# The first group's tokens gathered by halves, and eight instead of six step places in a layer's first expert pair

## What is computed

```
aff  = sigmoid(x @ router_w)                    # 16 experts in 4 groups of 4
g    = argmax of the groups' sum of their two best (aff + bias)
e    = the two best experts within group g; gate = aff[e] / sum(aff[e])
h    = silu(x @ w_gate[e]) * (x @ w_up[e]) * gate      # w_gate, w_up: 2048 x 512
out  = sum over the two experts of h @ w_down[e]       # w_down: 512 x 2048
x    = layer_norm(alpha * x + out)
```

## Time and profile before

| what | value |
|---|---|
| median of 3 runs | 1759.06 us (1756.92 to 1761.03) |
| the profiled execution | 1759.79 us, its span 1757.9 us |
| TensorE matmul busy | 1596.2 us, 91% |
| weight loads of TensorE | 948.4 us, 54% |
| VectorE, ScalarE, GpSimd busy | 720.8, 467.4, 16.8 us |
| moved by DMA | 538.12 MB, mean 306 GB/s |
| TensorE's mean granted clock | 0.977 of full |

### The profile page before, as it was taken

The page is one execution under the profiler, slowest core; times in us unless marked ns, Lnnn a source line. Parts: engine busy times, 40 slices in busy tenths (PEclk is TensorE's granted clock), DMA queues, the critical chain, the costliest instruction groups (busy, mean ns, idle before and its releaser), DMA issues.

```text
span 1757.9 us, 18363 instructions
## 1 busy us (share of the span) xinstructions
PE 1596.2 (91%) x7223; PEld 948.4 (54%) x7223; DVE 720.8 (41%) x1220; ACT 467.4 (27%) x693; POOL 16.8 (1%) x36
## 2 busy tenths in 40 slices
PE   8999999998999879898879999999799988989985
PEld 6888887876533224333237888878543323533321
DVE  6675555656211112111157797656521112111116
ACT  4565545432110001000024335553220000100000
POOL 1000000000000000000000000000000000000000
PEclk9999999998999999999999999999899999999998
DMA  8666554784899999999994555538489999999995
GB/s 267 174 180 182 166 158 141 262 310 157 319 416 421 421 416 422 419 422 421 421 361 120 168 167 162 162 121 347 175 354 421 421 421 416 421 415 422 421 419 234
DMA packets 133270, 538.12 MB, mean 306 GB/s; under 512 B 19377, under 2 KB 19505, under 8 KB 86849
## 3 DMA queue, kind: packets, MB, share of 16 engines
q1 hardware_dynamic: 132608, 532.75, 80.0%
q0 software_dynamic: 576, 4.19, 0.6%
HBM read 534.82 MB, written 2.10 MB: 305 GB/s over the span
## 4 chain that ended last, share of the span: by engine, by line
PE 56%; issue 29%; DMA 10%; DVE 3%; ACT 1%; SPq 1%; POOL 0%; POOLq 0%; DVEq 0%; ACTq 0%
PE ps L750 12%; PE ps L752 11%; PE ps L751 11%; PE ps L1035 8%; DMA ring<-in_moe_w_down 5%; PE ps L1097 4%; DMA ring<-in_moe_w_up 4%; PE ps L731 2%; PE ps L1015 1%; PE ps L1016 1%; PE ps L1024 1%; PE ps L1208 1%; PE ps L1222 1%; DMA arena<-in_x 0%; SPq L597 0%
## 5 line engine op out<-in xcount | busy, mean ns | idle before, releaser
L750 PE MATMUL ps<-w_lo,x_hi 128*128 128x512 f32 x880 | 350.7, 399 | 7.5 <-DVE x_lo L2312 2.5
L751 PE MATMUL ps<-w_hi,x_hi 128*128 128x512 f32 x880 | 344.7, 392 | 0.0
L1768 DVE TENSOR_TENSOR w_lo<-ring,w_hi 128x1024 fp32r<-128x1024 f32 x224 | 270.2, 1223 | 181.2 <-ACT w_hi L1315 179.6
L1315 ACT ACTIVATE w_hi<-ring 128x1024 fp32r<-128x1024 f32 x224 | 235.5, 1059 | 311.5 <-PE ps L752 306.8
L2210 DVE TENSOR_TENSOR arena<-ps,arena 128x512 f32<-128x512 f32 x128 | 82.9, 687 | 418.7 <-PE ps L1025 418.7
L750 PEld LDWEIGHTS ps<-w_lo,x_hi 128*128 128x128 f32 x880 | 166.5, 189 | 46.3 <-issue 7.2
L1035 PE MATMUL ps<-arena,hT 128*64 128x512 f32 x768 | 177.1, 616 | 9.6 <-DVE hT L2200 4.3
L751 PEld LDWEIGHTS ps<-w_hi,x_hi 128*128 128x128 f32 x880 | 166.5, 189 | 34.7 <-issue 0.5
L1097 PE MATMUL ps<-ring,arena 128*64 128x512 f32 x768 | 170.5, 594 | 6.4 <-DMA ring<-in_moe_w_down 6.4
L1524 ACT ACTIVATE y_hi<-ps 128x512 fp32r<-128x512 f32 x64 | 36.1, 596 | 459.9 <-PE ps L1097 239.7
L752 PE MATMUL ps<-w_hi,h_lo 128*128 128x512 f32 x384 | 150.2, 391 | 0.0
(11 more groups left out here) (333 smaller groups left out, 1530.8 us busy)
## 6 DMA issues: line engine op xcount, KB each, us to landing
arena<-in_moe_w_gate SPq DMA_DIRECT2D x48, 2048.0 KB, 18.3
ring<-in_moe_w_down SPq DMA_DIRECT2D x96, 1024.0 KB, 18.2
arena<-in_moe_w_up SPq DMA_DIRECT2D x32, 2048.0 KB, 20.4
ring<-in_moe_w_up SPq DMA_DIRECT2D x32, 2048.0 KB, 20.7
ring<-in_ab_w_in SPq DMA_DIRECT2D x96, 512.0 KB, 3.7
ring<-in_moe_w_gate SPq DMA_DIRECT2D x16, 2048.0 KB, 19.9
arena<-in_moe_w_down SPq DMA_DIRECT2D x32, 1024.0 KB, 17.1
ring<-in_c_w_in SPq DMA_DIRECT2D x64, 512.0 KB, 3.7
```

What stands on the lines that cost most here:

```text
L750: nc.tensor.matmul(t, x_h, w_l[:, k, :], start=(opens and k == 0), stop=False)
L751: nc.tensor.matmul(t, x_h, w_h[:, k, :], start=False, stop=False)
L1315: act.activation(high_unit(n), raw_unit(n)[0], ACT.Copy).then_inc(w_hi_ready, 1)
L1768: v.tensor_tensor(lo, raw, high_unit(n).bitcast(FP32), ALU.subtract).then_inc(w_lo_ready, 1)
```

## The change

Four edits, made together.

1. **Two more step places in a layer's first pair.** Steps 6 and 7 get places of their own in `arena` (words 0 to 4095 and 4096 to 8191); the steps after them go to place `(st - 2) % 6`. Steps 0, 7, 1 and 2 are loaded between the out projection's units, step 3 (layer 1: 4) after unit -5, and 4 (layer 1: 3), 5 and 6 after the last. Steps 0 and 1 of the second pair wait for steps 4 and 5 of the first instead of 6 and 7.
2. **The first group is gathered by halves.** 16 tiles with 256 columns for the first four experts go into `first_pairs` (all of `hT`); 16 tiles for the other four (`gather_rest`) go into `other_pairs` (words 0 to 4095 of `arena`, step 6's place): eight after the first pair's projections, and two before each two projections of the second pair.
3. **Picks by halves.** VectorE makes the picks of the first four experts first (`pick_first`), the others after `low(1, .)`; the first pair's picks are turned behind the second gather tile instead of before the first. A tile waits for its own token half of `h_lo`.
4. **Other homes.** The LayerNorm is done in place in `h`; the two vectors of the LN lie where `h_hi` will be; `acc` is formed later by VectorE as `h_hi + h_lo` (`acc_joined`) and scaled then by ScalarE. `mix_lo`, `attn_lo`, `rawT` and `rparts` move, and layer 1's units begin four slots later in `ring`, so that units 0 to 3 of layer 1 wait for step 6 of the last pair and units 4 to 7 for its step 11.

```diff
+        def opening(x):
+            return isinstance(x, int) and x == 0
+        def slot_of(x, st):
+            return st if opening(x) and st < 6 else (st - 2) % 6
...
-                if not (isinstance(x, int) and x == 0 and st < 6):
-                    sp.wait_ge(M[lay]["step_used"], STEPS * x + st - 5)
+                if not opening(x):
+                    sp.wait_ge(M[lay]["step_used"], STEPS * x + st - (7 if isinstance(x, int) and x == 1 and st < 2 else 5))
+                elif st >= 8:
+                    sp.wait_ge(M[lay]["step_used"], st - 7)
...
-                    if n in (UNITS[lay] - 12, UNITS[lay] - 8, UNITS[lay] - 4):
-                        sp.wait_ge(mix_ready if lay == 0 else mixer1_done, 1)
-                        load_step(lay, 0, 0, (n - UNITS[lay] + 12) // 4)
+                    if n in (UNITS[lay] - 12, UNITS[lay] - 9, UNITS[lay] - 6, UNITS[lay] - 3):
+                        load_step(lay, 0, 0, (0, 7, 1, 2)[(n - UNITS[lay] + 12) // 3])
+                early, late = (3, 4) if lay == 0 else (4, 3)
                 wait_unit_used(sp, lay, UNITS[lay] - RAW + 3)
-                load_step(lay, 0, 0, 3)
+                load_step(lay, 0, 0, early)
                 wait_unit_used(sp, lay, UNITS[lay] - 1)
-                for st in range(4, STEPS):
+                for st in (late, 5, 6, *range(8, STEPS)):
                     load_step(lay, 0, 0, st)
...
                     mine = slice(BANK * (k // 4) + k % 4, BANK * (k // 4 + 1), 4)
+                    n = HALF_GROUP if first else BANK
                     for tt in range(TT):
-                        nc.tensor.matmul(t, h_hi[:, tt, mine], pick8[:, tt, :], start=(tt == 0), stop=False)
+                        if first and k == 0:
+                            pe.wait_ge(s["pick_ready"] if tt else s["pick_begun"], 1)
+                        if first and k % 4 == 0:
+                            pe.wait_ge(s["h_lo_ready"], TT * (k // 4) + tt + 1)
+                        nc.tensor.matmul(t[:, 0:n], h_hi[:, tt, mine], pick8[:, tt, 0:n], start=(tt == 0), stop=False)
...
+                def gather_rest(k):
+                    b = k % 2
+                    pe.wait_ge(s["drained"][b], rest_at(k // 2))
...
+                        nc.tensor.matmul(t, h_hi[:, tt, mine], pick8[:, tt, HALF_GROUP:BANK], start=(tt == 0), stop=False)
+                        last = nc.tensor.matmul(t, h_lo[:, tt, mine], pick8[:, tt, HALF_GROUP:BANK], start=False, stop=(tt == TT - 1))
...
                             for k in range(4 * m, 4 * m + 4):
                                 gather_tile(g, first, k)
+                                if first and k == 1:
+                                    turn_pick()
...
+                        if first and i == 1:
+                            gather_rest(8 + 2 * m)
+                            gather_rest(9 + 2 * m)
...
+                    if first and i == 0:
+                        for k in range(8):
+                            gather_rest(k)
                     pe.wait_ge(s["h_ready"], x + 1)
...
-                pick_half(0, 0)
+                pick_first(0, 0).then_inc(s["pick_begun"], 1)
                 v.wait_ge(psum_full, filled(f"pos{lay}", 1))
...
-                pick_half(0, 1).then_inc(s["pick_ready"], 1)
+                pick_first(1, 0).then_inc(s["pick_ready"], 1)
                 low(0, 1)
                 norm(1)
                 for tt in range(TT):
                     low(1, tt)
+                for tt in range(TT):
+                    ins = pick_first(tt, 1)
+                ins.then_inc(s["pick_rest"], 1)
...
+                        v.wait_ge(s["h_lo_ready"], TT * 4)
+                        for tt in range(TT):
+                            v.tensor_tensor(acc[:, tt, :], h_hi[:, tt, :].bitcast(FP32), h_lo[:, tt, :].bitcast(FP32), ALU.add)\
+                             .then_inc(s["acc_joined"], 1)
```

More of the change, by code:

```diff
@@ L34 @@
 GPAIRS = GROUP // 2
+HALF_GROUP = GROUP // 2 * CAP
 STEPS = 12
 HALF = SLOT // 2
+OWN_PLACE = {6: 0, 7: SLOT}
 UNIT = 2 * BANK
@@ L283, in xc, with tokens_of @@
             return xc_lo[:, k, :] if k < KT // 2 else xc_hi[:, k - KT // 2, :]
+        first_pairs, _ = carve(hT_whole, 0, [KT, HALF_GROUP])
+        other_pairs, _ = carve(arena, 0, [KT, HALF_GROUP])
+        def tokens_of(first, i, k):
+            if not first:
+                return xc(k)[:, i * P:(i + 1) * P]
+            return (first_pairs if i < 2 else other_pairs)[:, k, i % 2 * P:(i % 2 + 1) * P]
         aff, k = carve(arena, xc_at, [TT, NE])
@@ L1105, in group @@
                 def group(g, first):
-                    pe.wait_ge(s["pick_ready"], g + 1)
+                    if not first:
+                        pe.wait_ge(s["pick_ready"], g + 1)
                     for i in range(GPAIRS):
@@ L1535, in pair @@
                         rows_hi(x - 1, 1)
+                    if not elder:
+                        gathered(g, first, 0)
                     act.wait_ge(s["pT_full"], x + 1)
@@ L1538, in pair @@
                     if i == 0:
-                        for k in range(0, 8, 2):
+                        for k in range(0 if elder else 2, 8, 2):
                             gathered(g, first, k)
@@ L1550, in pair @@
                         rows_hi(x - 1, 3, added[1])
+                    if first and i == 1:
+                        gathered_rest(12)
+                        gathered_rest(14)
                     act.wait_ge(s["step_used"], STEPS * x + 7)
                     act.activation(silu_g[:, :], ps[0][:, :], ACT.Silu).then_inc(s["silu_ready"], 1)
+                    if first and i == 0:
+                        for k in range(0, 8, 2):
+                            gathered_rest(k)
                     act.wait_ge(s["hT_full"], x + 1)
@@ L2223, in pair @@
                     if i == 0:
-                        for k in range(1, 8, 2):
+                        for k in range(1 if elder else 3, 8, 2):
                             gathered(g, first, k)
@@ L2233, in pair @@
                         add(0, at[0])
+                        if first and i == 1:
+                            gathered_rest(9)
                         rows_lo(x - 1, 2)
+                        if first and i == 1:
+                            gathered_rest(11)
                     if i == 0:
@@ L2242, in pair @@
                         rows_lo(x - 1, 3)
+                        if first and i == 1:
+                            gathered_rest(13)
+                            gathered_rest(15)
                         add(2, at[2])
@@ L2247, in pair @@
                     v.scalar_tensor_tensor(h_e[:, :], ps[1][:, :], comb_slot[:, 0:1], silu_g[:, :], ALU.mult, ALU.mult).then_inc(s["h_ready"], 1)
+                    if first and i == 0:
+                        for k in range(1, 8, 2):
+                            gathered_rest(k)
                     if i == GPAIRS - 1:
```

154 lines of the change are left out of this document (99 added, 55 removed).

## The result

The changed kernel takes 1770.56 us (median of 4 runs, 1768.65 to 1773.17), the kernel before 1759.09 (4 runs, 1756.92 to 1761.03): 1.0064 times as long, 95% interval 1.0049 to 1.0079. That is 11.5 us slower. The prediction, 1766.4, had the direction and the place; the time lies just inside its whole range (to 1771.0) and 1.6 us beyond the forecast's own (to 1769).

What follows compares the result with a forecast made beforehand. Expert stages are bound by loading expert weights; each layer's end hangs on when the queue is never dry again. Delays 3.4 + 4.0 = +7.4 us on 1759.79 give 1767.2, median 0.7 lower: 1766.4; range 1751.5 to 1771, forecast's own 1762.5 to 1769.

Steps and rivals of the forecast that it cites:

- the moment U: When TensorE has used step 8; the layer's end follows its shift, forecast +2.7 us in layer 0, +3.3 in layer 1.
- The price of a gather matmul, 0.225: One 256-column gather matmul was to take 0.225 us, paced by its strided weight load; bounds 0.118 and 0.24.
- Blocks: The three gather blocks after the first in a layer: each 0.8 us shorter, 2.4 in all.
- Rival A: Strided weight load hides after all, gather matmuls spaced 0.118 us: faster, 1752.3 us; chance 20%.
- point of decision, 0.19: Time per gather matmul under which the change wins, taken where the shift of U is zero: 0.19 us.
- Eight rest tiles, net +6.6: Second-half gathers between step 7's use and the hidden transposes: 7.4 us, hiding a 0.8 wait for h, net 6.6 later.
- First block, -1.5 and -0.9: Each layer's first gather block, until the first projection: 1.5 us gained in layer 0, 0.9 in layer 1.
- rival C: TensorE's clock may stay at 1.2 GHz into the first projections: 2 to 3.5 us a layer more, 1772; chance 10%.
- Second pair, step 18 +4.6: Step 18 issued about 4.6 us later, queue dry once more: layer 0 late by 3.4, layer 1 by 4.0.
- The rest stays covered: Steps after step 18 lose nothing more: step 20 ready at 522.4, before the queue needs it at 523.9.
- (b): Joining h_hi and h_lo on VectorE: 4.9 us at about 485, needed only after 501; counted as no cost.
- (a): Fourth step loaded among the out projection's units: counted as no cost; without ScalarE's cover, up to 1.5 us a layer.

Runs made afterwards that it cites:

- run 2: Changed kernel with the two own places for steps 6 and 7 removed, six places and the earlier load order: 1770.17 us, 1.0057.
- run 1: Changed kernel with 128 adjacent words of h as every gather's weights instead of every fourth word (output differs): 1749.53 us, 0.9942.
- Run 6: Changed kernel with only h_hi regrouped, so that half of the gather matmuls have adjacent weights: 1763.51 us, 1.0022.
- run 4: Changed kernel plus sixteen unused 512-column matmuls between the router's logits and the positions, where TensorE waited: 1770.16 us, 1.0055.
- run 8: Changed kernel plus the sixteen added matmuls of run 4 and twelve more in TensorE's holes between the first gathers: 1767.87 us, 1.0050.
- run 7: Kernel before the change with 128 adjacent words as weights of every gather (output differs): 1757.49 us, 0.9986.

## Why the prediction was right, and where it was short

- **The queue and the moment U.** Right. Step 14's issue moved by +3.6 in layer 0 and the layer by 3.7; run 2 shows the two places to be worth nothing; run 1 moved step 14 by the price of the loads and the time followed.
- **Luck in the number.** That layer 0 came out at 3.7 where 3.4 was forecast is chance: the clock's +1.8 was missed, and so was a gain of 1.6 in the out projection (both below), and they all but cancel. The 2.7 us that came back between the layers were in no term either. Without these two gains the same rows would give about 1775 (an estimate, 1770.6 + 1.6 + 2.7), beyond the whole range.
- **The price of a gather matmul, 0.225.** Right in kind (the load sets the pace), 0.237 measured, near the upper bound. The Trainium skill, "TensorE: Matmul & The Clock Gate", section "LDWEIGHTS (loading the stationary operand)", gives columns / 1.2 ns with no term for the step, an estimate of 107 ns here; run 1's spacing of 0.12 is near it (a load itself lasts 0.19), the changed kernel's 0.23 is not, and there the measurement decides. Blocks gained 0.65 each (443.74 to 448.31, 4.57 us) where 0.8 stood. Rival A's sum for 0.118, 1752.3, was confirmed by run 1's 1749.5 where the weights are adjacent. Its point of decision, 0.19, was somewhat high: a straight line from run 1 (0.12 us, 11.1 us under before) to the changed kernel (0.237, 11.5 over) crosses zero at about 0.18, an estimate. Run 6, at a mean of 0.177, was 0.2% slower than before, but with its dearer splits in it.
- **Eight rest tiles, net +6.6.** Measured 7.68 less 0.84, +6.8 (7.58 less 0.84, +6.7, in layer 1).
- **First block, -1.5 and -0.9.** From the last unit to the first projection 20.97 became 19.70 (-1.27), in layer 1 20.39 became 19.70 (-0.69).
- **The clock: this is the step that was mis-sized.** The forecast took the first two projections at the 7.09 of the earlier trace rows and left the clock to rival C. They took 8.92 in layer 0 and 9.70 in layer 1, +1.8 and +2.6, at a granted clock of 0.50 in the stretches in which they began. The sum of the four terms is then -1.3 + 1.8 - 2.0 + 6.8 = +5.3 (layer 1: -0.7 + 2.6 - 2.0 + 6.7 = +6.6) from the last unit; the rows show +5.2 and +6.5. Rival C, held at 10%, had named the mechanism and, with 2 to 3.5 us a layer, nearly the size; it came true on top of the forecast's other terms, not in place of them. Runs 4 and 8 show the cause: shorter gathers leave TensorE holes of up to 0.8 us (1.4 when its matmuls are faster) while it waits for the copies. With the 4.5 us wait for the router filled alone the clock falls at the first such hole, with both filled it stays up.
- **Second pair, step 18 +4.6.** Measured +4.5 in layer 0 (511.41), +8.7 in layer 1 (1343.75), where 1.1 of it was there at the last unit. The 513.0 at which the queue was to get to step 18 should have been 512.6 (487.64 + 2.7 + 2.35 + 4 x 4.98); 513.9 lies behind both.
- **"The rest stays covered".** Held in layer 0 but for 0.6 us (the lag went from 3.1 to 3.7 at 132 MB); in layer 1 it failed by 1.3 us, at the third pair's first steps (5-us window from 1385: 320 GB/s). TensorE was busy for 53.0 of the 55 us from 1340 to 1395, so next to nothing of a lateness was made up. The 0.7 us at 464 MB go back, as far as the rows tell, to the end of the first group: there the granted clock of the changed kernel was 0.66 for 1485 to 1490, and TensorE went from 10.0 us behind the kernel before (last projection of the group, 1479.74 against 1469.71) to 11.1 (last down step, 1502.49 against 1491.39). The kernel before was at 1.00 at that point of its work (1470 to 1495). Why the clock fell there isn't shown, nor whether it does in other executions. Of layer 1's 8.1 us, 4.0 were forecast; the clock's 2.6 and the 1.3 at the third pair make most of the difference.
- **Edits at nothing.** (b) right: the join took 4.48 us at 486.74, long before the first add. (a) the last unit of layer 1 was used at 1246.46, 1.1 after before's 1245.37, and just that lag stood there when layer 1's mixer began: no cost of its own that shows. Not foreseen: layer 0's last unit was used 1.6 us *earlier*, at 415.19 instead of 416.77. The matmul with mix_lo takes 389 ns at the median where it took 397; mix_lo moved in the arena. Run 2, with the load order of before, has 389 too, and run 7, which is the kernel before but for the gathers, has 397, so it isn't the order of the loads. Whether the address is the cause was not tried.
- **The last 1.2 us.** The vectors of the last normalisation are issued at 1732.99 instead of 1714.24, but that costs nothing: TensorE's projection that waits for the last pair's step 5 starts at 1711.44 against 1700.34, already 11.1 late, its last down step at 1743.03 against 1731.99 and the normalisation at 1755.71 against 1744.68, 11.0 both. So nothing is lost at the end. That the lag is 1.2 less when it is counted by the megabytes started (9.8) than by these waits stays open.

## What to carry to other kernels

Before halving a matmul's columns, look at the rows of its weight load: a load hidden behind 512 columns is bare behind 256, and one that reads every fourth word costs 0.23 us where an adjacent one costs 0.12. Lay the weights out adjacent first (here 0.4 us more a split on VectorE and ScalarE, taken off the critical path by order), then halve. And in a stage bound by its queue, more places or postponed work help only if the consumer has time to spare later; ask what TensorE's busy share is where the work is put.

## What was not expected of the hardware

- VectorE's and ScalarE's 512-column instructions went from 0.68 to 1.07 us and from 0.69 to 1.11 with a step of four words on the read side, and stay at 1.04 and 1.09 with the step (128 words) on the write side.
- In run 4 TensorE had been busy for most of 418 to 430 us at a clock of up to 1.00; one hole of 1.41 us went with a fall to 0.50 in the next window, and the gathers behind it did not bring it back.
